# Residual kept in PSUM at the inner norms of a two-block transformer kernel, sums of squares behind the third unit

## What is computed

```python
h = x
h = h + 0.5 * swiglu(rmsnorm(h, ffn1_norm), w_gate, w_up, w_down)      # ffn1
u = rmsnorm(h, mix_norm); ... = split(u @ w_in)                         # mix
h = h + sum(gates * proj(three attentions)) @ w_out
h = h + 0.5 * swiglu(rmsnorm(h, ffn2_norm), ...)                        # ffn2
z = rmsnorm(h, g_mix_2) @ w_in_2 + b_in_2                               # mix2
h = h + concat(conv(a * sigmoid(gate)), pool(p)) @ w_out_2
h = h + swiglu(rmsnorm(h, g_ffn_2), ...)                                # ffn3
return rmsnorm(h, g_final)                                              # final
```

## Time and profile before

| | |
|---|---|
| median of 3 runs | 1873.64 us (1872.53 to 1874.47) |
| the profiled execution | 1874.48 us, its span 1872.7 us |
| TensorE busy | 1803.2 us, 96% |
| VectorE, ScalarE, POOL busy | 44%, 34%, 43% |
| mean granted TensorE clock | 0.992 |

### The profile page before, as it was taken

The page is one execution under the profiler, slowest core; times in us unless marked ns, Lnnn a source line. Parts: engine busy times, 40 slices in busy tenths (PEclk is TensorE's granted clock), DMA queues, the critical chain, the costliest instruction groups (busy, mean ns, idle before and its releaser), DMA issues.

```text
span 1872.7 us, 23405 instructions
## 1 busy us (share of the span) xinstructions
PE 1803.2 (96%) x8538; PEld 1437.2 (77%) x8538; DVE 824.2 (44%) x1168; ACT 638.1 (34%) x982; POOL 809.0 (43%) x355
## 2 busy tenths in 40 slices
PE   7999999999999999999999999999898999999997
PEld 5888888867777766778878888888655788888885
DVE  4333340077877898557443333201415443333003
ACT  4232321263232444565343223221413533233122
POOL 4444444454444432324454444444422444444443
PEclk9999999999999999999999999999999999999998
DMA  4232232322333221112322223222341222222221
GB/s 170 95 101 90 100 100 92 129 84 86 118 102 118 68 68 35 46 46 79 101 80 100 97 94 101 92 99 90 96 127 53 90 79 101 98 92 101 91 100 56
DMA packets 51837, 171.62 MB, mean 92 GB/s; under 512 B 6840, under 2 KB 7352, under 8 KB 51648
## 3 DMA queue, kind: packets, MB, share of 16 engines
q1 hardware_dynamic: 45216, 160.27, 25.6%
q10 hardware_dynamic: 6560, 10.51, 2.0%
HBM read 161.83 MB, written 2.11 MB: 88 GB/s over the span
## 4 chain that ended last, share of the span: by engine, by line
PE 81%; DVE 13%; ACT 2%; issue 2%; DMA 1%; ACTq 1%; POOL 0%; DVEq 0%; SPq 0%
PE bank L441 24%; PE bank L443 24%; PE bank L442 24%; PE bank L623 4%; PE bank L784 2%; DVE input_low L1201 2%; DVE top_keys L1404 2%; DVE top L1403 1%; PE bank L668 1%; DVE head_root L1340 1%; PE bank L694 1%; DVE top_keys L1445 1%; DVE residual L1237 1%; DVE tile L1432 1%; PE bank L566 1%
## 5 line engine op out<-in xcount | busy, mean ns | idle before, releaser
L378 POOL TENSOR_TENSOR weights_low<-raw_weights,weights_high 128x1024 fp32r<-128x1024 f32 x296 | 731.5, 2471 | 1043.3 <-ACT weights_high L877 1043.2
L877 ACT CAST weights_high<-raw_weights 128x1024 fp32r<-128x1024 f32 x296 | 311.4, 1052 | 938.6 <-PE bank L443 880.5
L441 PE MATMUL bank<-input_high,weights_high 128*128 128x512 f32 x1488 | 592.7, 398 | 29.3 <-DVE input_low L1201 21.4
L442 PE MATMUL bank<-input_high,weights_low 128*128 128x512 f32 x1488 | 583.2, 392 | 0.0
L443 PE MATMUL bank<-input_low,weights_high 128*128 128x512 f32 x1488 | 583.0, 392 | 0.0
L441 PEld LDWEIGHTS bank<-input_high,weights_high 128*128 128x128 f32 x1488 | 281.5, 189 | 105.0 <-issue 23.8
L443 PEld LDWEIGHTS bank<-input_low,weights_high 128*128 128x128 f32 x1488 | 281.6, 189 | 59.8
L442 PEld LDWEIGHTS bank<-input_high,weights_low 128*128 128x128 f32 x1488 | 281.7, 189 | 59.0 <-issue 2.6
L441 PE MATMUL bank<-hidden_high,weights_high 128*128 (+1 forms) x528 | 205.6, 389 | 0.0
L443 PE MATMUL bank<-hidden_low,weights_high 128*128 (+1 forms) x528 | 205.5, 389 | 0.0
L442 PE MATMUL bank<-hidden_high,weights_low 128*128 (+1 forms) x528 | 205.5, 389 | 0.0
(11 more groups left out here) (215 smaller groups left out, 1681.3 us busy)
## 6 DMA issues: line engine op xcount, KB each, us to landing
raw_weights<-weights SPq DMA_DIRECT2D x296, 512.0 KB, 3.4
glu_stacked<-glu ACTq DMA_DIRECT2D x64, 64.0 KB, 2.1
tile<-tile ACTq DMA_DIRECT2D x36, 64.0 KB, 2.4
residual<-x_t SPq DMA_DIRECT2D x4, 512.0 KB, 8.7
out_t<-out_t SPq DMA_DIRECT2D x8, 256.0 KB, 2.2
mem_in<-mem_t ACTq DMA_DIRECT2D x1, 1024.0 KB, 5.8
tile<-forget_sums ACTq DMA_DIRECT2D x4, 256.0 KB, 3.5
rope_cos<-forget_sums ACTq DMA_DIRECT2D x2, 256.0 KB, 4.2
```

Source lines behind the costliest of these rows:

```text
L378: pool.tensor_tensor(wl[:, u % SPL, :], raw[:, u % RAW, :], wh[:, u % SPL, :].bitcast(F32), ALU.subtract).then_inc(low_done, 1)
L441: pe.matmul(out, wh[:, u % SPL, w], rh, start=start, stop=False)
L442: pe.matmul(out, wl[:, u % SPL, w], rh, start=False, stop=False)
L877: act.copy(wh[:, u % SPL, :], raw[:, u % RAW, :]).then_inc(high_done, 1)
```

## The change

It touches the four inner norms, and for the place of the sums also the first one.

- VectorE's addition writes bank m in PSUM in place of the residual. ScalarE's high part and VectorE's low part read the bank. Then ScalarE copies the bank to the residual (`keep`). TensorE waits for copies 0 and 1 at the pair's two units and for all eight behind the pair.
- ScalarE's order is new: high parts 0 to 7 with copies 0 to 5 among them, the cast of the third unit, copies 6 and 7, squares 0 to 4 (with the cast of the fourth unit behind square 2). VectorE makes squares 5 to 7 itself and adds all eight (`add_all_squares`); POOL adds none at these norms.
- The second unit of the pair runs 4 chunks behind the first. The sums stand behind the third unit, the spreading in the middle of the fourth (behind its fourth chunk). At the first norm too.
- The projections of both mixers turn over four banks (bank 3 is new; the convolution has bank 2 for it) and may run three takes ahead. In the first mixer what followed the third unit follows the fourth and fifth, two forgetting steps of TensorE one step later.
- On ScalarE the first pair of `gate_up` no longer issues the casts of the third and fourth unit, except at ffn1, where both stand ahead of the root. The cast of the fifth unit keeps its place behind the first pair's silu and high copy. In the mixers the first two casts are likewise gone from the steps.

The diff, cut to its core:

```diff
-        proj = [bank[0], bank[1], bank[7]]
+        proj = [bank[0], bank[1], bank[7], bank[3]]
-        conv_banks, maps = [bank[3], bank[6]], bank[4:6]
+        conv_banks, maps = [bank[2], bank[6]], bank[4:6]
...
-            def project(u, out, rh, rl, low_at, n=S):
+            def project(u, out, rh, rl, low_at, n=S, factor_of=None):
                 pe.wait_ge(low_done, low_at)
                 for k in range(DK):
+                    if factor_of and k == BK:
+                        spread_factor(factor_of)
...
+                lag = 3 if name == "ffn1" else 4
...
                             pe.wait_ge(low_done, unit + 1)
+                            if name != "ffn1":
+                                pe.wait_ge(sem("residual_kept"), keeps(name, unit - u0))
...
-                sums(name)
+                if name != "ffn1":
+                    pe.wait_ge(sem("residual_kept"), keeps(name, DK - 1))
...
                 pair_start(feed, u0, bank[0][:, :], bank[1][:, :])
-                spread_factor(feed)
                 project(u0 + 2, bank[2][:, :], xh, xl, u0 + 3)
-                project(u0 + 3, bank[3][:, :], xh, xl, u0 + 4)
+                sums(feed)
+                project(u0 + 3, bank[3][:, :], xh, xl, u0 + 4, factor_of=feed)
...
+            def feed_high(name, gain, m):
+                act.wait_ge(sem("residual_added"), added(name, m))
+                act.activation(xh[:, m, :], bank[m][:, :], ACT.Copy, scale=v(gain, m)).then_inc(sem("input_high"), 1)
+            def keep(name, m):
+                act.wait_ge(sem("input_low"), fed(name, m))
+                act.copy(h[:, m, :], bank[m][:, :]).then_inc(sem("residual_kept"), 1)
             def feed(name, gain, u_last):
+                feed_high(name, gain, 0)
+                feed_high(name, gain, 1)
+                keep(name, 0)
+                feed_high(name, gain, 2)
+                after(u_last)
+                feed_high(name, gain, 3)
+                keep(name, 1)
+                for m in range(4, DK):
+                    feed_high(name, gain, m)
+                    keep(name, m - 2)
+                after(u_last + 1)
+                keep(name, DK - 2)
+                keep(name, DK - 1)
+                for m in range(ACT_SQUARES):
+                    feed_square(name, m)
+                    if m == 2:
+                        after(u_last + 2)
...
                     for c in range(2):
-                        after(u0 + 2 * c, i)
-                        if c == 0 and i is None:
+                        if c or i is not None:
+                            after(u0 + 2 * c, i)
+                        else:
+                            if feed_name == "ffn1":
+                                after(u0)
+                                after(u0 + 1)
                             feed_root(feed_name, bank[4])
-                            after(u0 + 1)
                         one = (0 if i is None else i * 2) + (c + 1)
                         act.wait_ge(sem(f"{name}_gate"), one)
...
+            def add_all_squares(name):
+                for m in range(ACT_SQUARES, DK):
+                    dve.wait_ge(sem("residual_kept"), keeps(name, m))
+                    dve.tensor_tensor(tiles[m][:, :], h[:, m, :], h[:, m, :], ALU.mult).then_inc(sem("late_square"), 1)
+                for m in range(1, DK):
...
+                    dve.tensor_tensor(tiles[0][:, :], tiles[0][:, :], tiles[m][:, :], ALU.add
+                                      ).then_inc(sem("squares_totalled"), 1)
...
-                    dve.scalar_tensor_tensor(out=h[:, m, :], in0=bank[m][:, :], scalar=share,
+                    dve.scalar_tensor_tensor(out=bank[m][:, :] if parts else h[:, m, :], in0=bank[m][:, :], scalar=share,
                                              in1=h[:, m, :], op0=ALU.mult, op1=ALU.add
...
-                        low(name, gain, m - 1)
+                        low(name, gain, m - 1, bank[m - 1][:, :])
```

More of the change, by code:

```diff
@@ L282, in added, with keeps, squared, late @@
             return fed(name, m) - DK
+        def keeps(name, m):
+            return added(name, m)
         def squares(name):
-            return (INPUTS.index(name) + 1) * (POOL_SQUARES - 1) + (DK - 1) * (name not in ("ffn1", "mix"))
+            return POOL_SQUARES - 1 if name == "ffn1" else 2 * (POOL_SQUARES - 1) + DK - 1
+        def squared(name, m):
+            return sum(DK if n in ("ffn1", "final") else ACT_SQUARES for n in INPUTS[:INPUTS.index(name)]) + m + 1
+        def late(name, m):
+            return (INPUTS.index(name) - 1) * (DK - ACT_SQUARES) + m - ACT_SQUARES + 1
+        def totalled(name):
+            return sum(DK - POOL_SQUARES if n in ("ffn1", "final") else DK - 1
+                       for n in INPUTS[:INPUTS.index(name) + 1])
         def nth(name):
@@ L330, in build @@
         LAST = max(SPLITS) + 1
-        POOL_SQUARES = 5
+        POOL_SQUARES, ACT_SQUARES = 5, 5
         MEM_STEP = 0
@@ L468, in pair_start @@
             def pair_start(name, u0, out0, out1):
-                for k in range(DK + 3):
-                    for unit, out, c in ((u0, out0, k), (u0 + 1, out1, k - 3)):
+                lag = 3 if name == "ffn1" else 4
+                for k in range(DK + lag):
+                    for unit, out, c in ((u0, out0, k), (u0 + 1, out1, k - lag)):
                         if not 0 <= c < DK:
@@ L822, in _ @@
             for j in range(2, len(IN2_STEPS)):
[L823 to L825 removed]
+                if j >= 4:
+                    pe.wait_ge(sem("in2_taken"), j - 3)
+                project(U_IN2 + j, proj[j % 4][:, :], xh, xl, U_IN2 + j + 1, factor_of="mix2" if j == 3 else None)
                 if j == 2:
[L827 to L828 removed]
+                    sums("mix2")
                 if j in CONV_AFTER:
@@ L900, in feed @@
                         after(u_last)
-                    act.wait_ge(sem("residual_added"), added(name, m))
-                    feed_chunk(name, gain, m)
+                    act.wait_ge(sem("residual_added"), added("final", m))
+                    feed_chunk("final", None, m)
             def take_gates(n):
@@ L915, in stepped @@
                     if j < n_steps:
-                        after(U_IN + j)
+                        if j >= 2:
+                            after(U_IN + j)
                         if j == 0:
@@ L1146, in _ @@
             for j, kind in enumerate(IN2_STEPS):
-                after(U_IN2 + j)
+                if j >= 2:
+                    after(U_IN2 + j)
                 if j == 0:
@@ L1183, in _ @@
             down(U_DN3)
-            feed("final", None, UNITS - 1)
+            feed_final(UNITS - 1)
             feed_root("final", bank[4])
@@ L1240, in feed @@
                     if parts and m:
-                        low(name, gain, m - 1)
+                        low(name, gain, m - 1, bank[m - 1][:, :])
                 if parts:
-                    low(name, gain, DK - 1)
+                    low(name, gain, DK - 1, bank[DK - 1][:, :])
             def gate_up(name, u0):
@@ L1369, in _ @@
             for m in range(DK):
-                low("ffn1", "ffn1_norm", m)
+                low("ffn1", "ffn1_norm", m, h[:, m, :])
             dve.wait_ge(sem("constants_loaded"), 16 * 4)
```

60 lines of the change are left out of this document (32 added, 28 removed).

## The result

The changed kernel takes 1911.51 us (median, 1910.78 to 1913.14) where the kernel before took 1874.06 beside it: 1.0203 times as long, 95% interval 1.0187 to 1.0219, or 37.5 us more. The forecast was 30.8 more. The time lies in the stated range, and the profile shows the case that was called the likeliest, with a loss 6.7 us larger than forecast. The profiled execution's span is 1911.1 us, 38.4 more than before.

The account below looks back on a forecast made before the run. The prediction took TensorE, busy 96% of the span, as the bound. Feed-forwards 11.5, first mixer 3.1, second mixer 6.8 and clock 9.4 gave +30.8 us on the profiled 1874.48, a median of 1904.4; range 1884 to 1913.

Parts of the forecast that it names:

- the case that was called the likeliest: Whole kernel: the forecast itself, +30.8 us to a median of 1904.4, given a chance of 0.62.
- input_low from PSUM is not blocked: Inner norms: VectorE's low part, reading one operand from PSUM, takes 0.68 to 0.70 us unblocked, where 2.34 stood.
- The pair: Inner norms: the first two units take 12.0 us, 3.1 saved at each of four; third unit starts at 12.15.
- The block by POOL: Inner norms: POOL's low parts hold up VectorE operations with two SBUF inputs; TensorE waits 2.6 us at the sums.
- The cast in the queue: Feed-forwards: ScalarE's cast for the fifth unit, behind the first pair's silu and high copy, makes TensorE wait 4.4 us.
- Mixers: Work hanging on the later spreading: first mixer +3.1 us; second +6.8, its GLU wait 12.9 in place of 4.4.
- The clock: TensorE's granted clock falls towards the 1.2 GHz level behind new waits, costing 9.4 us together.
- The 1.0 for the later squares of mixer 1: First mixer: VectorE's steps begin 7.2 us later, TensorE's fifth unit 2.1; late squares taken to cost 1.0.
- Rival (a): Inner norms: POOL doesn't hold VectorE long enough to matter, no wait at the sums; +16.3, 1890 us; chance 0.20.
- Rival (b): Feed-forwards: the cast for the fifth unit is not late, so the kernel gets faster: 1858 us; chance 0.08.
- Rival (c): Inner norms: input_low still waits for POOL, or ScalarE is slower from PSUM; pair saves nothing; +12.4, 1917 us; chance 0.06.
- (d): About equal: squares in time, no clock loss, other work covers the second mixer's taps; 1873 to 1877 us; chance 0.04.

## Why the prediction was right, point by point

- **input_low from PSUM is not blocked**: right. Its mean over the inner norms is 0.747 us, the longest near 0.75, where 2.34 stood; forecast 0.68 to 0.70. The price in the Trainium skill, "VectorE: DVE Perf Modes", section on the TRN2 errata (62 cycles more for a PSUM source) is an estimate of 0.065 and would fit the difference to 0.683. But in this profile the shortest input_low with the residual in SBUF, at the first norm, takes 0.740, so the source in PSUM is not what lengthened it. The trace does not show that price.
- **The addition into PSUM**: forecast 0.68, measured 0.694.
- **The pair**: forecast 12.0 long and the third unit at 12.15; measured 12.33 and 12.85. VectorE's chunks 3 and 4 came 0.08 later than forecast, and the triples behind a wait are slower than 0.68. The cast of the third unit then started at 9.18 in place of 8.65, its low part ended at 12.70, and TensorE waited 0.36 for it. The prediction had no wait there. So each inner norm is 0.7 late at the third unit, 2.8 us at four.
- **The block by POOL**: right. Sums forecast at 20.2 with a wait of 2.6, measured 20.95 and 2.40. The Trainium skill's rule, "SBUF — State Buffer", section "Who interferes with whom", agrees with the trace (one square and one addition at this norm held until POOL ended), and the run with the sum in PSUM shows its other half: additions with one input in PSUM ran at 0.697 on the mean beside POOL, with both in SBUF at 0.987.
- **The cast in the queue**: right. Forecast wait 4.4 at three norms, measured 4.45, 4.49 and 4.46; fifth unit of the first norm forecast at 45.5, measured 44.92. That one is partly luck: the load at the start was 0.96 shorter in this profile, and counted from the pair's start the fifth unit came 0.4 later than forecast.
- **Mixers**: fifth unit of the first forecast at t0 + 32.65, measured 33.05; the GLU's wait forecast 12.9, measured 12.52.
- **The clock: the term that was mis-sized most.** "So a new wait of 4.4 costs 1.7 more, three of these 5.1; of 2.6, half of that, four times 3.4; the one in mixer 1 0.9" gave 9.4 where the runs show 14.2. The fifth unit of ffn2 and the stretch behind the sums there:

```profile
990.00:992.00 2.00, 2.00 (x6) 1.71 (x7) 0.18 (x1) 1.55 (x2) 0.00 (x0) 0.50 0.00 0
992.00:994.00 2.00, 2.00 (x6) 1.52 (x6) 0.00 (x0) 0.00 (x0) 0.00 (x0) 0.50 0.00 0
994.00:996.00 2.00, 2.00 (x8) 1.61 (x7) 0.00 (x0) 0.00 (x0) 0.00 (x0) 0.54 0.00 0
...
1005.00:1007.00 2.00, 2.00 (x6) 1.61 (x5) 1.75 (x1) 0.10 (x1) 1.68 (x1) 0.50 0.83 254
1007.00:1009.00 2.00, 2.00 (x6) 1.52 (x6) 0.23 (x1) 0.00 (x0) 0.00 (x0) 0.50 0.56 180
```

(Stretch in us; busy of PE, PEld, DVE, ACT, POOL; granted clock; DMA.) The clock stood at 0.50, the 1.2 GHz level. Behind the wait of 4.49 the first six triples took 6.80 us, where six by 0.68 are 4.08: 2.7 are lost. In the same way 2.7 are lost at ffn1, 2.5 at ffn3 and, behind the 3.03, 1.7 in the first mixer. From the start of the sums to the spreading it took 6.77 at ffn2 and 5.33 at ffn3, but 3.73 in either mixer with the same wait of 2.4: 3.0 and 1.6 are lost, and nothing twice. Together these are 14.2. The 1.7 of the prediction was read from the taps, and they are another kind of work: even behind the wait of 12.5 the first 64 took 8.71, as they had behind 4.39 (8.75).
- **The sum.** The fifth unit, counted from its pair's start and without what the clock took at the sums, was forecast to come later by 5.0, 2.1, 3.4, 6.8 and 3.1 us (ffn1, mixer 1, ffn2, mixer 2, ffn3) and came later by 5.3, 2.5, 4.5, 7.3 and 4.1: 23.7 for 20.4. The 1.0 for the later squares of mixer 1 became 1.7, and the clock took 14.2 for 9.4. Mixer 2 made up 0.3 behind its fifth unit, and the load at the start was 1.0 shorter. Together that is 38.3, and the span grew by 38.4. By stage (from one pair's start to the next, the first from the start of the span) it is ffn1 7.1, mixer 1 6.0, ffn2 10.3, mixer 2 7.0, ffn3 8.1. Nearly all the errors have one sign, so the total is not near because errors cancelled.

Rival (a), squares in time, fell with the wait of 2.4 at all four norms. The run with the sum in PSUM is what it would have looked like, and it took 1900.5 us, not the 1890 that (a) was priced at. Rival (b) fell with the cast: not even with both causes mended (1886.0) did the order of this change come below the kernel before. Rival (c) fell with input_low; (d) with the taps.

## What to carry to other kernels

Moving a reduction later to cover its latency moves everything that hangs on its result. Before counting the wait saved, list for each in-order queue what stands behind the first instruction that needs the result, casts and transfers of other work too. Here, where VectorE worked beside POOL, one operand in PSUM kept it free (0.70 to 0.75 us an operation); but the squares and additions that the detour gave to VectorE had both inputs in SBUF, and two of them at each norm took over 2.5. Mending one of two linked waits brought 7.4 or 11.0 us, mending both 25.5, so test them together before a theory is given up.

## What was not expected of the hardware

The same wait of 2.40 us at the sums, in the same place of each inner norm, was followed by a granted clock of 0.50 from about 989 to 996 us at ffn2, for half as long at ffn3, and by no such stretch in either mixer:

```profile
406.00:408.00 2.00, 2.00 (x14) 1.80 (x15) 0.18 (x1) 0.66 (x2) 0.00 (x0) 1.00 0.00 0
408.00:410.00 2.00, 2.00 (x12) 1.73 (x11) 0.00 (x0) 0.00 (x0) 0.00 (x0) 1.00 0.00 0
```

(the first mixer, behind its wait that ended at 405.84). In length the waits do not differ, so the length of a wait alone does not price it. That the wait had a part in it is shown by the run with the sum in PSUM: there the sums of ffn2 waited 0.37, and the granted clock from them to the spreading was 1.00. What decides between the four was not tried.
